# Scan of an SSD mixer: a difference tile of 128 rows, memory rounding, C·B products and gating moved in the order of work

## The reference

```
# first block
z, xbc, dt_f, dt_b, q, k, v, gates = split(rms_norm(x) @ w_in)
xs, b_in, c_in = split(silu(conv(xbc)))            # 4 groups of 8 heads, head width 64, state 128
y = ssd(xs, dt_f, ...) + flip(ssd(flip(xs), ...)) + d_skip * xs
y = group_rmsnorm(y * silu(z), ssd_norm_g)         # a group is 512 wide
x = x + (g_ssd * (y @ w_br_ssd) + g_attn * (attn @ w_br_attn)) @ w_out
x = x + memory_cross_attention(rms_norm(x), rms_norm(mem), w_q, w_kv, w_o)
x = x + swiglu_ffn(rms_norm(x))
# second block: ffn, gated recurrence with a short convolution, cross attention with mem_2, ffn, final norm
```

## Time and profile before

| | us |
|---|---|
| median of 3 runs | 2633.09 (2632.88 to 2635.0) |
| profiled execution, its own time | 2637.43 |
| its span | 2635.6 |
| PE busy | 2514.1 (95%) |
| VectorE (DVE) busy | 1324.4 (50%) |
| ScalarE (ACT) busy | 934.2 (35%) |
| GpSimd (POOL) busy | 483.3 (18%) |

### The profile page before, as it was taken

One profiled execution on the slowest core, in us unless ns is written; L12 is line 12 of the kernel. 1 busy time (PEld: TensorE's weight loads), 2 busy tenths in 40 slices (PEclk: granted clock), 3 DMA queues, 4 the chain that ended last, 5 costly groups with the idle time before them and its releaser, 6 DMA issues.

```text
span 2635.6 us, 29123 instructions
## 1 busy us (share of the span) xinstructions
PE 2514.1 (95%) x11378; PEld 2008.5 (76%) x11378; DVE 1324.4 (50%) x1955; ACT 934.2 (35%) x1489; POOL 483.3 (18%) x329
## 2 busy tenths in 40 slices
PE   6999899999798999999999999999999999999997
PEld 5766567776667788788888888888887787888886
DVE  3788855445666544444443354333377654434422
ACT  4334334333445423333333233322444243333221
POOL 2422100043330001021111111101255311111101
PEclk9999999999898999999999999999999999999998
DMA  5411124431334623133332233333321231333331
GB/s 161 122 57 56 40 88 137 136 104 57 104 117 124 228 91 120 56 96 97 96 96 88 93 92 99 100 105 96 98 62 58 78 104 62 92 100 100 97 103 48
DMA packets 173258, 254.20 MB, mean 96 GB/s; under 512 B 11840, under 2 KB 88896, under 8 KB 173120
## 3 DMA queue, kind: packets, MB, share of 16 engines
q1 hardware_dynamic: 173120, 252.33, 30.3%
HBM read 231.83 MB, written 16.78 MB: 94 GB/s over the span
## 4 chain that ended last, share of the span: by engine, by line
PE 78%; DVE 10%; issue 5%; ACT 3%; POOL 1%; DMA 1%; SPq 1%; DVEq 0%; ACTq 0%; POOLq 0%
PE bank L974 77%; DVE T L1694 2%; DVE W L1686 1%; POOL acc L2403 1%; ACT pr L1369 1%; DVE pr L1690 1%; DVE T L1691 1%; ACT whi L1277 0%; DVE wlo L1686 0%; DVE pr L1804 0%; PE bank L1054 0%; DVE stg L1694 0%; DMA scr_z<-T 0%; DVE SC L2317 0%; DVE E L1686 0%
## 5 line engine op out<-in xcount | busy, mean ns | idle before, releaser
L974 PE MATMUL bank<-xh,whi 128*128 128x512 f32 x1784 | 722.4, 405 | 22.5 <-DVE wlo L1686 17.8
L1686 DVE TENSOR_TENSOR wlo<-raw,whi 128x1024 fp32r<-128x1024 f32 (+1 forms) x354 | 436.9, 1239 | 568.6 <-ACT whi L1277 568.5
L974 PE MATMUL bank<-xh,wlo 128*128 128x512 f32 x1784 | 701.5, 393 | 0.0
L974 PE MATMUL bank<-xl,whi 128*128 128x512 f32 x1784 | 701.3, 393 | 0.0
L1277 ACT ACTIVATE whi<-raw 128x1024 fp32r<-128x1024 f32 (+2 forms) x406 | 416.1, 1038 | 538.7 <-PE bank L974 532.5
L974 PEld LDWEIGHTS bank<-xh,whi 128*128 128x128 f32 x1784 | 339.1, 190 | 120.9 <-issue 31.3
L974 PEld LDWEIGHTS bank<-xh,wlo 128*128 128x128 f32 x1784 | 338.5, 190 | 72.9
L974 PEld LDWEIGHTS bank<-xl,whi 128*128 128x128 f32 x1784 | 339.4, 190 | 70.3 <-issue 3.8
L974 PE MATMUL bank<-hh,whi 128*128 128x512 f32 x528 | 205.4, 389 | 0.0
L974 PE MATMUL bank<-hl,whi 128*128 128x512 f32 x528 | 205.4, 389 | 0.0
L974 PE MATMUL bank<-hh,wlo 128*128 128x512 f32 x528 | 205.4, 389 | 0.0
(11 more groups left out here) (341 smaller groups left out, 3643.7 us busy)
## 6 DMA issues: line engine op xcount, KB each, us to landing
raw<-in_w_in SPq DMA_DIRECT2D x92, 512.0 KB, 3.7
raw<-in_w_ffn_in SPq DMA_DIRECT2D x88, 256.0 KB, 3.3
raw<-in_ffn_gate SPq DMA_DIRECT2D x88, 256.0 KB, 2.8
raw<-in_ffn_up SPq DMA_DIRECT2D x88, 256.0 KB, 3.1
raw<-in_ffn_down SPq DMA_DIRECT2D x44, 512.0 KB, 3.5
raw<-in_w_ffn_out SPq DMA_DIRECT2D x22, 512.0 KB, 3.5
raw<-in_w_xattn_kv SPq DMA_DIRECT2D x16, 512.0 KB, 3.7
raw<-in_w_kv_mem SPq DMA_DIRECT2D x16, 512.0 KB, 4.1
```

Source lines behind the costliest of these rows:

```text
L974: return e.matmul(out, l, r, start=start, stop=stop, skip_group_check=skip)
L1686: return e.tensor_tensor(out, a, b, op)
```

## The change

- `dTs` and `idd` get 128 rows. `dif` holds the 32 heads four times (128 columns) and lies elsewhere. Rows 64 to 127 of `idd` are zero (columns 0 to 31 of the unit matrix's lower half), so rows 64 to 127 of `dTs` are multiplied by zero.
- `dif` is written by VectorE right behind `nac` in `cum`, and the transposition is asked for three scan steps after `cum` instead of one.
- The `cb` products and their copies are put before `cum`; what VectorE does with them for the skip term is a step of its own, `skip`.
- `y_scale` becomes `y_mean` (one `soon` point later: mean and root) and `y_scale` (three points: reciprocal and scaling).
- Memory 1 and memory 2 have buffers of their own, placed on parts of `xh` and `xl` that z3 has finished with; the low part is written over the loaded memory. `prepare` runs beside the block before: memory 1 beside z3 (loads after 16 of its steps, two steps a tile; the roundings beside the last four tiles), memory 2 beside `mkv12` and `mkv13` (one step a tile). The three scan steps without tiles are gone.
- At the end of the scan each transposition is followed by one open gating, and `gs_load` comes four steps after the last gating, beside `bs0`.

```diff
@@ -155,8 +155,8 @@
         E = [at_kb(118 + 2 * i, [P, 4, P], name="E") for i in range(2)]
-        dTs, idd = at_kb(122, [64, S], F32R, name="dTs"), at_kb(124, [64, 32], F32R, name="idd")
-        dif = at_kb(125, [P, 4, 64], name="dif")
+        dTs, idd = at_kb(122, [P, S], F32R, name="dTs"), at_kb(124, [P, 32], F32R, name="idd")
+        dif = at_kb(138, [P, 4, P], name="dif")
         even = at_kb(126, [P, 4, S], name="xk")
@@ -178,9 +178,10 @@
-        mt = at_kb(72, [P, 8, 256], name="mt")
-        mh, ml = at_kb(80, [P, 8, 256], F32R, name="mh"), at_kb(88, [P, 8, 256], F32R, name="ml")
-        macc = at_kb(96, [P, 256], name="macc")
+        mt = {i: at_kb(64 + 8 * i, [P, 8, 256], name="mt") for i in (1, 2)}
+        ml = {i: at_kb(64 + 8 * i, [P, 8, 256], F32R, name="ml") for i in (1, 2)}
+        mh = {i: at_kb(80 + 8 * i, [P, 8, 256], F32R, name="mh") for i in (1, 2)}
+        macc = at_kb(125, [P, 256], name="macc")
         xq = at_kb(118, [P, 8, S], name="xq")
...
@@ -601,7 +603,8 @@
             if c == 3:
-                step("y_scale", g)
+                soon(1, "y_mean", g)
+                soon(3, "y_scale", g)
@@ -633,20 +636,23 @@
             step("dt")
-            for _ in range(7):
+            for g in range(4):
+                yield
+                side.new("cb", g)
+                step("cb", g)
+            for _ in range(3):
                 yield
             step("cum")
+            for g in range(4):
+                yield
+                if g == 2:
+                    side.new("dT")
+                    step("difference")
+                tmp.new("skip", g)
+                step("skip", g)
             yield
-            side.new("dT")
-            step("difference")
-            yield
-            for g in range(4):
-                side.new("cb", g)
-                tmp.new("cb", g)
-                step("cb", g)
-                yield
             yield from groups(0, 1)
@@ -683,21 +689,22 @@
-        scan = start(ssd(), 2.9)
-        for g in range(4):
-            gemm(f"z{g}", ev_z(g))
-
-        def memory(tag, runs):
-            step("mark", f"mem{tag}")
+
+        def prepare(tag, points):
+
+            for _ in range(points):
+                yield
             for k in range(8):
                 step("m_load", tag, k)
-            for _ in range(3):
-                if runs in beside and next(runs[0], "end") == "end":
-                    beside.remove(runs)
+            for _ in range(7):
+                yield
             for k in range(8):
                 step("m_split", tag, k)
-            for k in range(8):
                 square(f"m{tag}", k)
+                soon(1, "m_lo", tag, k)
+                yield
+
+        def memory(tag):
             late.append(norm(f"m{tag}", lag=2, among=ELSE))
@@ -707,10 +714,18 @@
             gemm(f"mkv{tag}1", ev("mk_out", 1))
+            if tag == 1:
+                start(prepare(2, 0), 4)
             gemm(f"mkv{tag}2", ev("mv_out", 0))
             gemm(f"mkv{tag}3", ev("mv_out", 1))
-        memory(1, scan)
-        memory(2, scan)
+
+        scan = start(ssd(), 2.9)
+        for g in range(4):
+            if g == 3:
+                start(prepare(1, 16), 8)
+            gemm(f"z{g}", ev_z(g))
+        memory(1)
+        memory(2)
         drain(scan)
@@ -720,18 +735,26 @@
                     yield
+                if posts:
+                    fetch_z()
+                    post()
             step("x_again")
             next(turns)
-        while posts:
-            fetch_z()
-            post()
-        step("mark", "post")
-        step("gs_load")
         start(turns, 4)
+
+        def ev_late():
+
+            while posts:
+                yield
+            for _ in range(4):
+                yield
+            step("mark", "post")
+            step("gs_load")
+        start(ev_late(), 4)
@@ -1125,7 +1148,7 @@
                 for c in range(4):
-                    ins = e.transpose(b[0:64, chunk(c)], dif[:, c, :], ident)
+                    ins = e.transpose(b[:, chunk(c)], dif[:, c, :], ident)
                 ins.then_inc(*up("cum", ("dT",)))
@@ -1139,7 +1162,7 @@
                         for j in range(2):
-                            mm(b[:, chunk(j)], dTs[:, chunk(2 * half + j)], idd[:, n:n + 1].to_broadcast([64, P]),
+                            mm(b[:, chunk(j)], dTs[:, chunk(2 * half + j)], idd[:, n:n + 1].to_broadcast([P, P]),
                                False, True, skip=True)
...
@@ -1480,9 +1503,10 @@
                 copy(idd[0:32, :], cst[0:32, 0, 0:32]).then_inc(*up("scan_act", ("idd half",)))
-                copy(idd[32:64, :], cst[32:64, 0, 32:64]).then_inc(*up("scan_act", ("idd",)))
+                copy(idd[32:64, :], cst[32:64, 0, 32:64]).then_inc(*up("scan_act", ("idd half",)))
+                copy(idd[64:128, :], cst[64:128, 0, 0:32]).then_inc(*up("scan_act", ("idd",)))
                 w.wait_ge(*at("dT"))
-                copy(dTs[:], b[0:64, :]).then_inc(*up("scan_act", ("dT hi",)))
+                copy(dTs[:], b[:]).then_inc(*up("scan_act", ("dT hi",)))
@@ -1512,15 +1536,14 @@
-            def y_scale(g):
+            def y_mean(g):
                 w.wait_ge(*at("y mean", g))
                 u, b = side("yturn", j)
-                label = "ssd" if j < 3 else "post"
                 for other in ("pe", "dve", "pool"):
-                    w.wait_ge(*at(other, label))
+                    w.wait_ge(*at(other, "ssd"))
                 w.wait_ge(*at("y turn", j))
@@ -1532,9 +1555,8 @@
             def m_split(tag, k):
-                w.wait_ge(*at("pe", f"mem{tag}"))
                 w.wait_ge(*at("m in", f"m{tag}", k))
-                copy(mh[:, k, :], mt[:, k, :], V("mem" if tag == 1 else "mem_2", k)).then_inc(
+                copy(mh[tag][:, k, :], mt[tag][:, k, :], V("mem" if tag == 1 else "mem_2", k)).then_inc(
                     *up("m_hi", ("m hi", tag, k)))
...
@@ -1950,6 +1972,10 @@
                 tt(nac[:], nac[:], acu[:], ALU.subtract).then_inc(*up("cum_dve", ("nac",)))
+                w.wait_ge(*at("nac"))
+                for i in range(4):
+                    ins = tt(dif[:, :, 32 * i:32 * i + 32], nac[:, :, 0:32], nac[:, :, 32:64], ALU.subtract)
+                ins.then_inc(*up("cum_dve", ("dif",)))
                 w.wait_ge(*at("tot"))
...
@@ -1985,10 +2011,6 @@
             def difference():
-                w.wait_ge(*at("nac"))
-                for i in range(2):
-                    ins = tt(dif[:, :, 32 * i:32 * i + 32], nac[:, :, 0:32], nac[:, :, 32:64], ALU.subtract)
-                ins.then_inc(*up("cum_dve", ("dif",)))
                 u, b = side("dT")
@@ -2049,10 +2071,13 @@
-            def y_scale(g):
+            def y_mean(g):
                 s = ss[:, 4 * g:4 * g + 4]
                 ts(s, s, 1.0 / 512, EPS, ALU.mult, ALU.add).then_inc(*up("y_scaled", ("y mean", g)))
+
+            def y_scale(g):
+                s = ss[:, 4 * g:4 * g + 4]
                 w.wait_ge(*at("y sqrt", g))
@@ -2084,10 +2109,11 @@
-            def m_split(tag, k):
+            def m_lo(tag, k):
                 w.wait_ge(*at("m hi", tag, k))
-                stt(ml[:, k, :], mt[:, k, :], V("mem" if tag == 1 else "mem_2", k), mh[:, k, :].bitcast(F32), ALU.mult,
-                    ALU.subtract).then_inc(*up("m_lo", ("x lo", f"m{tag}", k)))
+                w.wait_ge(*at("square", f"m{tag}", k))
+                stt(ml[tag][:, k, :], mt[tag][:, k, :], V("mem" if tag == 1 else "mem_2", k),
+                    mh[tag][:, k, :].bitcast(F32), ALU.mult, ALU.subtract).then_inc(*up("m_lo", ("x lo", f"m{tag}", k)))
...
@@ -2422,7 +2448,9 @@
                     return
-                label = {"m1": "mem1", "m2": "mem2", "mix": None, "fb2": "fad"}.get(tag) or RES.get(tag, [None])[0]
+                if tag == "m2":
+                    w.wait_ge(*at("rms sum", "m1"))
+                label = {"m1": "ba", "m2": "ba", "mix": None, "fb2": "fad"}.get(tag) or RES.get(tag, [None])[0]
                 if label:
@@ -2638,13 +2666,9 @@
             def m_load(tag, k):
-                if tag == 1:
-                    w.wait_ge(*at("w used", G["z3"]["ids"][1]))
-                else:
-                    w.wait_ge(*at("square", "m1", k))
-                    w.wait_ge(*at("x lo", "m1", k))
+                w.wait_ge(*at("w used", G["z3"]["ids"][1 if tag == 1 else 3]))
                 src = io["memT" if tag == 1 else "memT_2"]
-                e.dma_start(mt[:, k, :], src[chunk(k), :]).then_inc(*up(f"mx{k}", ("m in", f"m{tag}", k)))
+                e.dma_start(mt[tag][:, k, :], src[chunk(k), :]).then_inc(*up(f"mx{k}", ("m in", f"m{tag}", k)))
```

More of the change, by code:

```diff
@@ L294, in build @@
         OPERAND["o"] = [oh[:, k, :] for k in range(8)], [ol[:, k, :] for k in range(8)]
-        OPERAND["m1"] = OPERAND["m2"] = [mh[:, k, :] for k in range(8)], [ml[:, k, :] for k in range(8)]
+        for i in (1, 2):
```

(13 more changed lines are left out.)

## The result

| kernel | median, us | runs |
|---|---|---|
| before | 2634.05 | 2632.88 to 2635.97 |
| after | 2610.19 | 2603.77 to 2612.77 |

What follows compares the result with a forecast made beforehand. TensorE, busy 95% of the span, was taken as the bound. Terms 16 + 4.5 + 4.4 + 4.9 + 7.1 + 12 - 7 = 42 us gave 2591 us; range for 8 in 10: 2568 to 2617.

Steps and rivals of the forecast that it cites:

- the tile's work: 64 `seg` calls: with 128 rows each falls from 0.79 to 0.48 us, 20 us of PE work saved.
- rival B: Padded tile gives little, the time being the matmul's own or eaten by DVE and ACT: 2607 us, chance 0.20.
- The discount on it: Tile's saving counts only where PE does not wait: 0.8 of 20 us, so 16 us.
- C·B ahead of the cumulation: `dif` follows `nac` at once, so PE's wait on `dif` goes: 4.5 us.
- The gatings and the memories: Waits taken off: 4.4 us (`xg`, second group) and 4.9 (`yl`) by the gatings, 7.1 (`ml`) by the memories.
- The clock: Half-clock windows, 526 to 894.7 us: full clock would take up to 23.9 us less; half taken, 12 us.
- Crowding: ACT and DVE beside z3's last tiles, plus an unhidden DVE chain at `bs0`'s start: 7 us lost (0 to 15).
- rival D: Slower: ACT's crowding delays freeing of `seg`'s banks, about 15 calls waiting 3.3 us each: 2634 to 2640 us, chance 0.05.
- Rival E: Preparation's waits move into z3's tail with their length and the tile gives nothing: 2626 to 2633 us, chance 0.08.
- those on `seg`, `dif`, `ml` and `yl`: Signs: `seg` call 0.46 to 0.50 us, no PE wait on `dif`, `ml` under 1 us, `yl` under 2.
- That on the root: Sign: no PE wait of over 2 us where `ss` is rooted.
- those on the stage: Signs: PE's busy share over 0.92, fewer than 30 us at half clock, stage about 370 us instead of 412.

## Why the prediction was right or wrong

**Right.** The direction, the range, and the tile's work, which was the first term: 20 us priced, 19.2 measured in the stage (19.3 with the tile alone). Its mechanism is the one named, the loads that now start ahead. That the size fits so well is in part luck: a call was priced at four times 0.12, and in the one shown the pair takes 0.17 and not 0.24, the 256 columns behind it 0.175 and not 0.12. The Trainium skill (TensorE: Matmul & The Clock Gate, LDWEIGHTS) gives a 32-row and a 128-row load the same time, and for the length of the load the trace agrees: 0.29 us for the pair with 64 rows, 0.30 with 128. What the rule leaves out is when the load starts, and that was the gain; as rival B it is refuted. The Trainium skill (TensorE: Matmul & The Clock Gate, "Wait — 56ns, not 53.3ns?") has back-to-back matmuls of 128 columns start every 55.6 ns at full clock, and the pair's two starts, 0.055 us apart, agree; from the second to the matmul behind it is 0.11. The matmul behind the pair, too, went from 0.22 to 0.175, since its load no longer starts with it.

**The discount on it was too small.** I took 0.8 of the saving as time. The tile alone brought 12.4 of 19.3, 0.64 of it: the rest came back as idle time (51.3 instead of 42.7), at the same queues.

**C·B ahead of the cumulation: 4.5 predicted, nothing measured.** The failed step is the sentence that `skip` has "no PE step behind it until `skip_x`". It has one: the copy of the first state waits for a mark set behind it. The tile with C·B is at 0.9961, the tile alone at 0.9953, a loss of 2 us that is inside the intervals.

**The gatings and the memories: 16.4 predicted (4.4 + 4.9 + 7.1), 14.7 measured together.** The two do not compare, since the measured one has the crowding and the clock in it: with these 21.4 were predicted. The parts are not right either: they overlap, and the memories alone bring all. Of the waits, `ml` went and `yl` fell from 4.9 to 2.7 in all, as said (4.9 again without the gatings' move); that on `xg` behind the root of the second group stayed at 4.2, so its 4.4 were priced and not won. And what went with `ml` came back at z3's end: PE stands 14.6 us around the first memory, before and after. What the memories' move does bring is in good part the clock.

**The clock: 12 predicted, 3.9 measured in the trace, about 5 by the granted clock of all runs.** This is the largest miss of a term. The step that failed is "I take half": it counts the low stretches as a consequence of waits that go, and does not reckon with the waits that come. The longest stretch after, 13.6 us, lies on the new waits for `T` and `HF`, and another one at 658 us on that for `E`. Whether the tile itself has a part in it, since PE with less work waits more, is open: in eleven traces with the tile of 128 rows the loss in the stage is 20 to 29 us and in the one of the order without it 15, but over all runs the order alone and the whole change have the same time at half clock (102 and 104 us).

**Crowding: 7 lost predicted.** It is there, where it was put: 7.5 us on `E` at z3's end, rival D's mechanism in small. It struck once and not 15 times, so D was far off. In that place `E` is named for 10.2 us (7.5 for ScalarE, 2.7 for VectorE) and not for over 15. There is no new low stretch at the start of the SSD branch.

So against 42: the tile 12.4 (16), C·B 0 (4.5), gatings and memories 14.7 with their crowding and clock in it (16.4 + 12 - 7 = 21.4). That is 27; with C·B at its measured loss of 2 it is the 25 of the ratio. B's number came near only because the misses have its size. Rival E's claim, that waits move with their length, holds for C·B and for the first memory, and the wait behind the second group's root, now at 743, stayed as long as it was. Two readings of the rows were off as well and carry little: the low stretches were nine and not eight, and of the 42.7 us that PE lacks the two places named hold half (13.4 and 7.9), not most.

Of the signs that were to show it, those on `seg`, `dif`, `ml` and `yl` came true (0.46 us in the call shown, though 0.54 in the median one). That on the root did not, with 4.2 and 3.5 us on `xg` where none over 2 was to be. And those on the stage did not: PE's share of it is 332.9/375.7 = 0.89 and not 0.92, 58 us at half clock and not under 30, and 23 us less and not 42.

## What to carry to other kernels

Split a stage into the bounding engine's work at full clock, its loss to the low clock and its idle time, before and after: a saving of work is safe in the first and came back in part as idle time, so waits should not be priced as if the work stayed. Take the clock's part from the granted clock of all runs: between single traces it differed by 7 us where the code was the same. When a wait is taken away, follow the next instruction's waits too, marks set behind a whole group of steps among them, and don't add up the gains of edits that shorten the same queue. And a stationary operand of 64 rows among 128-row ones was worth padding here, 12 us for 64 calls, though the added rows count for nothing.

## What was not expected of the hardware

- Between 128-row matmuls a pair of fp32r matmuls of 128 columns takes 0.055 us to its second start and 0.11 from there to the next matmul with 128 rows; with 64 rows these were 0.16 and 0.20, with loads of the same length, the first of which starts late. 96 rows go as 128 do.
- The load of a 128-row operand starts 0.11 us ahead of its own matmul while another 128-row matmul is running (698.50, during the one started at 698.49).
